# Expert products of a mixture-of-experts block: which operand stands still in TensorE

## What is computed

```python
def expert_block(args):
    xb, e = args                      # xb: 128 rows of 1024 features
    return (jax.nn.silu(xb @ w1[e]) * (xb @ w3[e])) @ w2[e]
```

## Time and profile before

| what | us |
|---|---|
| median of 3 executions (lowest, highest) | 2008.15 (2003.61, 2013.16) |
| the profiled execution | 2005.71 |
| its span, first to last instruction | 2003.9 |
| TensorE busy in the span | 1737.4 (87%) |
| VectorE busy | 1236.5 (62%) |
| ScalarE busy | 913.3 (46%) |
| GpSimd busy | 360.1 (18%) |
| mean granted TensorE clock | 0.943 of full |

### The profile page before, as it was taken

How to read it: one execution, slowest core, us unless ns; L and a number is a source line. 1 busy time by engine, 2 the same in 40 slices (tenths; PEclk the granted TensorE clock), 3 DMA queues, 4 the chain that set the end, 5 groups by cost and what they waited for, 6 DMA issues and landing times. The chain is left out here.

```text
span 2003.9 us, 36549 instructions
## 1 busy us (share of the span) xinstructions
PE 1737.4 (87%) x14653; PEld 1451.4 (72%) x14653; DVE 1236.5 (62%) x1634; ACT 913.3 (46%) x1304; POOL 360.1 (18%) x423
## 2 busy tenths in 40 slices
PE   1799999799969997999977989728999999999950
PEld 1578888687858885988866868616888888888840
DVE  5733254540104446677744455468999999999948
ACT  2521111122115554444422132116888888888833
POOL 2000011100020000112120001111333333333316
PEclk9999999899989998999998999859999999999985
DMA  8455556541136441101025313274899999999927
GB/s 293 142 183 190 175 203 219 193 161 43 47 90 152 101 85 52 43 27 51 9 99 223 117 56 116 84 310 194 348 382 390 385 391 385 381 379 381 381 105 290
DMA packets 116031, 393.53 MB, mean 196 GB/s; under 512 B 24720, under 2 KB 31888, under 8 KB 94400
## 3 DMA queue, kind: packets, MB, share of 16 engines
q1 hardware_dynamic: 84304, 324.01, 43.8%
q0 software_dynamic: 16848, 41.38, 5.8%
q10 hardware_dynamic: 14752, 26.29, 3.5%
HBM read 341.22 MB, written 67.18 MB: 204 GB/s over the span
## 5 line engine op out<-in xcount | busy, mean ns | idle before, releaser
L2359 DVE TENSOR_TENSOR ex_w_r<-w,ex_w_r 128x1024 fp32r<-128x1024 f32 x384 | 451.0, 1219 | 24.4 <-ACT ex_w_r L2301 11.1
L2301 ACT ACTIVATE ex_w_r<-w 128x1024 fp32r<-128x1024 f32 x384 | 403.4, 1062 | 109.2 <-PE psum L2240 86.3
L270 PE MATMUL psum<-w_hi,h_hi 128*128 128x512 f32 (+1 forms) x576 | 222.4, 386 | 13.1 <-ACT stage L477 13.1
L272 PE MATMUL psum<-w_hi,h_lo 128*128 128x512 f32 (+1 forms) x576 | 221.3, 384 | 0.0
L271 PE MATMUL psum<-w_lo,h_hi 128*128 128x512 f32 (+1 forms) x576 | 221.3, 384 | 0.0
L2238 PE MATMUL psum<-ex_w_r,ex_x_t 128*128 128x512 f32 x512 | 204.1, 399 | 4.0 <-DVE ex_x_t L2359 2.4
L2240 PE MATMUL psum<-ex_w_r,ex_x_t 128*128 128x512 f32 x512 | 201.2, 393 | 0.0
L2239 PE MATMUL psum<-ex_w_r,ex_x_t 128*128 128x512 f32 x512 | 201.2, 393 | 0.0
L477 ACT ACTIVATE stage<-psum 128x512 f32<-128x512 f32 (+1 forms) x72 | 41.3, 574 | 320.9 <-PE psum L272 190.6
L270 PEld LDWEIGHTS psum<-w_hi,h_hi 128*128 128x128 f32 x576 | 109.2, 190 | 37.7 <-ACT stage L477 7.9
L359 DVE TENSOR_TENSOR w_lo<-w_ring,w_hi 128x4096 fp32r<-128x4096 f32 (+1 forms) x11 | 46.5, 4228 | 130.9 <-ACT w_hi L430 130.9
(11 more groups left out here) (377 smaller groups left out, 3714.4 us busy)
## 6 DMA issues: line engine op xcount, KB each, us to landing
w<-in_exp_w SPq DMA_DIRECT2D x128, 1024.0 KB, 13.8
w<-in_exp_w SPq DMA_DIRECT2D x32, 2048.0 KB, 9.4
w_ring<-in_ada_w SPq DMA_DIRECT2D x12, 2048.0 KB, 10.5
w_ring<-in_w_in SPq DMA_DIRECT2D x10, 2048.0 KB, 10.3
qk<-stage_r ACTq DMA_DIRECT2D x16, 512.0 KB, 2.8
gates<-stage ACTq DMA_DIRECT2D x32, 256.0 KB, 2.3
bl_gates<-gates SPq DMA_DIRECT2D x8, 1024.0 KB, 4.9
w<-pair_rows SPq DMA_DIRECT2D x8, 1024.0 KB, 17.1
```

The lines of the kernel that those rows point to most:

```text
L270: nc.tensor.matmul(out, a_hi, b_hi, start=(i == 0), stop=False)
L272: last = nc.tensor.matmul(out, a_lo, b_hi, start=False, stop=(i == n - 1))
L2301: return nc.scalar.activation(out, src, ACT.Copy)
L2359: return nc.vector.tensor_tensor(out, whole, high.bitcast(F32), ALU.subtract)
```

## The change

The first two products take the split weights as the stationary operand, 128 features at a time, and the activations (128 rows) as the moving one. The result stands by features: in bank 2 + j the columns f*128 to f*128+127 hold features f*128+p on partition p, for 128 rows. The four transposes of `ex_hidden`, and the waits ahead of them, are gone; ScalarE and VectorE read `ex_hidden` in SBUF in place of bank 4; L2388 writes in the order in which it reads. `w2` is laid out with feature k*128+p on partition p to match, so a partition reads four pieces of 4 KB. The third product is as it was.

```diff
 def load_down(nc, sp, sig, keep, ins, par, e):
-    sp.dma_start(keep["w2"][:, par], src.rearrange("(p k) n -> p k n", k=FE // P)).then_inc(sig(f"w2_in{par}"), 16)
+    sp.dma_start(keep["w2"][:, par], src.rearrange("(k p) n -> p k n", p=P)).then_inc(sig(f"w2_in{par}"), 16)
...
                     for j in range(2):
-                        last = product(bank[2 + j], [x_t[:, par, i, k, :] for i in range(2)], k,
-                                       slice(j * FE, (j + 1) * FE), k == 0, k == KT - 1)
+                        for f in range(FK):
+                            cols = slice(j * FE + f * P, j * FE + (f + 1) * P)
+                            w_hi, w_lo = w_r[:, k % RING, 0, cols], w_r[:, k % RING, 1, cols]
+                            x_hi, x_lo = x_t[:, par, 0, k, :], x_t[:, par, 1, k, :]
+                            features = bank[2 + j][:, f * P:(f + 1) * P]
+                            nc.tensor.matmul(features, w_hi, x_hi, start=(k == 0 and f == 0), stop=False)
+                            nc.tensor.matmul(features, w_hi, x_lo, start=False, stop=False)
+                            last = nc.tensor.matmul(features, w_lo, x_hi, start=False, stop=(k == KT - 1 and f == FK - 1))
                     last.then_inc(sig("up_used"), 1)
...
-                pe.wait_ge(sig(f"hidden{par}"), pair + 1)
-                if before:
-
-                    pe.wait_ge(sig(f"hid_lo{before[0]}"), before[1] + 1)
-                for k in range(FK):
-                    last = nc.tensor.transpose(bank[4][:, k * P:(k + 1) * P], hidden[:, k * P:(k + 1) * P], ident[:])
-                last.then_inc(sig(f"hid_flipped{par}"), 1)
...
-                act.wait_ge(sig(f"hid_flipped{par}"), pair + 1)
-                copy(hid_t[:, par, 0].rearrange("p k t -> p (k t)"), bank[4]).then_inc(sig(f"hid_hi{par}"), 1)
+                act.wait_ge(sig(f"hidden{par}"), pair + 1)
+                copy(hid_t[:, par, 0].rearrange("p k t -> p (k t)"), hidden[:]).then_inc(sig(f"hid_hi{par}"), 1)
...
-                nc.vector.tensor_tensor(hidden[:].rearrange("p (k q) -> p q k", k=FK), bank[3].rearrange("p (q k) -> p q k", k=FK),
-                                        sigm[:].rearrange("p (q k) -> p q k", k=FK), ALU.mult).then_inc(sig(f"hidden{par}"), 1)
+                nc.vector.tensor_tensor(hidden[:], bank[3], sigm[:], ALU.mult).then_inc(sig(f"hidden{par}"), 1)
...
-                low(parts[1], bank[4], parts[0]).then_inc(sig(f"hid_lo{par}"), 1)
+                low(parts[1], hidden[:], parts[0]).then_inc(sig(f"hid_lo{par}"), 1)
```

## The result

The changed kernel takes **2359.8 us** (median of 4 runs, 2356.0 to 2364.5) where the kernel before takes 2006.7 (median of 4): ratio 1.174, 95% interval 1.172 to 1.177. The forecast was 2324, the range 2285 to 2365. The profiled execution took 2355.99, its span 2354.1.

A forecast was written before the change was run, and what follows sets the result against it. PE was taken to set the pace. Per block 21.50 - 11.00 - 0.36 = +10.14 us, over 32 blocks +324.5, with the late gather's -6 +318.5, on the profiled 2005.71: 2324 us, range 2285 to 2365.

The forecast's parts named there:

- The slot: One block's turn in the experts' steady part, forecast at 27.8 us where it was 17.69.
- turn of the slot: Ring's first unit ready just in time for the next products; if 0.3 us late, 10 us on top.
- Matmuls: First two products: 192 load-and-matmul steps a block at 0.112 us, 21.50 us for 11.00; ends 0.055 and 0.118.
- Rival A: In the first two products loads run wholly beside matmuls: step 0.055 to 0.060, 1993 us; chance 0.04.
- Rival B: In the first two products loads are cheaper or w_hi loads once for two matmuls: 2095 or 2158 us; chance 0.07.
- Flips of hidden: Four transposes a block leave PE's path: 0.36 us a block saved.
- DVE and ACT: Contiguous ex_hidden write saves DVE 0.4 us, SBUF reads cost the same within 0.1; all hidden behind PE.
- loads: The w2 transfers in 4 KB pieces for 16 KB stay hidden, as DMA has 27.8 us a block for 17.0 busy.
- The late gather: One gather, waited for 4.52 us before, comes in time once slots are longer: -6 us, once.
- Clock: Granted TensorE clock stays at 1.00 in the new products, as in the attention stage; cost nothing.
- Rival C: Clock drops to the 1.2 GHz level in the new products, steps double: about 2980 us; chance 0.05.
- the prediction's sign "clock 1.00": Sign that the forecast is right: clock 1.00; 0.5 or between in the experts' stage would show it wrong.

The follow-up runs named there:

- e7: Changed kernel with two matmuls for three in the first two products (high weights loaded once for high and low rows), VectorE adding the halves: 2210.6 us.
- e8: Changed kernel with extra 512-column float32 matmuls at the experts' start: 8 before and 5 behind the first transposes, 8 at the first slot's end: 2324.4 us.
- e6: Kernel before with the new w2 layout and plain ex_hidden write, and the fourth block's gather issued before the first block's store: ratio 0.9967 (2002.7 us).
- e1: Changed kernel with 22 extra float32 matmuls of 512 columns, 16 before and 6 behind the experts' first transposes: 2352.3 us.

## Why the prediction was right, and where its sum was short

The slot was right to 0.06 us, and that is 322.6 of the 353. But the time fell into the range by luck: it lies 36 us above the forecast, the room up to 2365 was there for a step of 0.118 and a late turn of the slot, and neither came. What filled it was a term that the sum had at nothing, the clock.

*Matmuls.* Right. 0.112 a step was taken, 0.111 measured; 21.39 us a block for 21.50. The ends, 0.055 and 0.118, were not needed. That the load sets it was argued from L637; the three sizes show it. The Trainium skill's 81 ns for 128 columns (TensorE: Matmul & The Clock Gate, section Back-to-back issue gap) was not seen: 111 ns here. The same page of the Trainium skill, section LDWEIGHTS, gives a load's time in ns as its columns divided by 1.2; an estimate from it is 107 ns for 128. The 111 at the full clock come near it, but at the low level the step was 214, so here a load goes with the clock and is not a fixed 107.

*Rival A*, loads hidden: refuted; only the first step behind the third product goes at 0.06. *Rival B*: three matmuls with w_hi twice in a row take three steps of 0.111, so the same weights are loaded again; with one load for both e7 took 2210.6 where the forecast of that case was 2095, which lacked the wait for VectorE (2.4 a slot, 77 us), had the pair at 0.224 for 0.231 (14 us), and had no falls of the clock (13 us in three pairs of slots). That makes 2199; the other 11 us are not accounted for.

*Flips of hidden.* 0.36 a slot was taken, 0.45 measured by putting them back; small.

*DVE and ACT, loads, turn of the slot.* Right: 0.69 for ex_hidden where 0.68 was taken, the w2 layout free, the ring's first unit 0.3 us ahead.

*The late gather.* The 6 us were right, and so was that longer slots would cover it; in the changed kernel the first two were longer still (41 us of products), but with the clock kept up (e8) the gather is in time too. "The gathers lie under less traffic" was no reason: e6 shows that it was the queue.

*Clock.* This is the step that failed: "I cost the clock at nothing". The row behind it, clock 1.00 in the attention stage, was of a stretch where the clock was already up. Nothing in it told of a start from the low level, which the experts' stage has: the earlier trace rows has the transposes at 1.97 us behind a wait, which the prediction took for the late gather and for what a low clock costs, without asking where else the clock is low. The term was 0 and measured 35 us (e8 against the changed kernel; 34.9 from the slots). With it the forecast's 2324 would be 2359. Put the other way, the kernel with the clock kept up takes 2324.4, which was the number forecast; to that digit it is chance, since this kernel still pays some 5 us for its extra matmuls and the forecast carried the 4.3 that the kernel before loses at its own start. Rival C had a low clock, but as a fall in all 32 slots, 650 us. In the changed kernel it was low in two slots only, and the prediction's sign "clock 1.00" failed there.

## What to carry to other kernels

The operand that leaves the longer moving side to the other should stand still. In a row, each fp32r matmul with 128 stationary columns (and each float32 one, 0.112 in L637) costs at least 0.11 us here for its load, also where its stationary operand is that of the matmul before it. With 64 or 128 moving columns the array waits for loads, and only from 256 on (0.120 a step) is most of the step used. Before such a change count loads, not multiplications, and look for a stretch of the trace with short matmuls in a row; its second step can flatter, read the third. And when a change makes matmuls short, ask not only whether the clock will hold but how it gets up: at each start and behind each wait a stage may need some long matmuls, and without them the step was twice as long (0.214 for 0.111) for as long as the short stream lasted.

## What was not expected of the hardware

- The stream of 128 x 128 matmuls neither raises nor drops the clock: at 0.50 for 42 us and more (a wait lay between), and at 1.00 for 21 us in every later slot. With 64 moving columns it dropped in every slot from the third on. With 256 it rose within 10 us of the first product, and so it did with 128 moving but 64 stationary columns.
- The wait of 3.6 us at the end of the first slot was enough for a fall when that slot had run at the full clock (e1); filled with long matmuls there was none (e8). A wait of 2.4 us in every slot was followed by a fall in some slots and not in others (e7: six of the 29 behind the first two). Why in these isn't known.
- With 256 and 128 moving columns in turn the starts are 0.17 and 0.06 apart, while the loads start 0.11 and 0.12 apart; the sum is what was expected, and why the matmuls' starts are uneven is not explained by any run.
- Slots of e6 are 17.73 us for 17.69 of before, in both kernels with the earlier gather; 1.3 us in all. Its cause wasn't looked for.
